# Two PSUM banks per head take turns under the attention scores of short query tiles

## The chip, the cores and the metric

The kernel runs on one core of one Trainium2 chip. The core has TensorE (PE; its weight loads are shown apart as PEld), VectorE (DVE), ScalarE (ACT), GpSimd (POOL), SyncE (SP) and DMA queues. Each engine has its own list of instructions, which it works through in the order written; semaphores are all that ties one engine to another. PSUM, into which TensorE writes, has eight banks of 512 float32 columns by 128 partitions. The metric is the device time of one execution in microseconds (us); smaller is better.

## The reference

One layer of a hybrid decoder trunk for two groups of requests: a prompt of 1024 tokens and eight sequences of four new tokens each. An input projection feeds an mLSTM group and a native-sparse-attention (NSA) group; their gated outputs are joined, projected and added back. The change is in the NSA part of the prompt. Cut to what matters:

```
scale = N_HEAD_DIM ** -0.5            # 64
s_c = einsum(q, k_compressed) * scale; p_c = masked_softmax(s_c)    # 64 compressed blocks
s_s = einsum(q_rot, k_selected) * scale; p_s = masked_softmax(s_s, pos_s <= t)
s_w = einsum(q_rot, k_window) * scale; p_w = masked_softmax(s_w, 0 <= t - s < 512)
out = g0 * (p_c @ v_c) + g1 * (p_s @ v_s) + g2 * (p_w @ v_w)
```

There are 8 query heads on 2 key/value heads of 64 dimensions. With 1024 prompt tokens there are 16 selection blocks of 64 and the top 16 are taken, so the selected branch is causal attention over everything up to the query. The window branch looks back 512 tokens.

## The kernel before

The whole kernel is one hand-ordered program per engine: projections of the prompt and the mLSTM recurrence (to about 560 us), compression of keys and values, the attention loop over the prompt (590 to 872 us), the part for the eight sampled sequences (to about 1070 us), and the output projection.

**Tiling of the attention loop.** The prompt is cut into 8 query tiles of 128 tokens. Each tile has 8 pairs; a pair p = 8i + 4br + g is tile i, branch br (0 selected, 1 window) and query head g of each of the two key/value heads h = 0, 1. Helper `pair(p)` gives nb, the number of 128-token key blocks: i + 1 for the selected branch, at most 5 for the window branch. So pairs 0 to 31 (tiles 0 to 3) have 1, 2, 3 and 4 blocks, and all from pair 32 on have five to eight.

**One pair, engine by engine.**
- TensorE, `scores(p)` (L2007 on): for each head one matmul of up to 512 key columns, from 64 of the 128 rows of the array (head 0 the lower, head 1 the upper), into the head's own PSUM banks, 2h and, above four blocks, 2h + 1 (L2019). A float32 matmul shows as two instructions, so a group for both heads is "x4". Then a small bf16 matmul adds the causal mask (L2025) and raises `s_done`.
- VectorE, `max_of` (L1515): the row maximum, negated, from PSUM.
- ScalarE, `exps` (L1134): exponentials from PSUM into SBUF `pp[p % 2][h]`, with the row sum, which is read out by a short instruction of its own (ACTIVATION_READ_ACCUMULATOR); this raises `s_exp`.
- VectorE, `scale` (L1524, L1526): reciprocal of the sum, then multiplication with it and the gate.
- TensorE, `turn_weights(p, h)` (L2038): one 128 x 128 transpose per block, into banks 4 and 5 in turn. ScalarE, `take_turned` (L1147), copies them to SBUF.
- TensorE, `values` (L2051): products with the values, accumulated in bank 6 over a tile. VectorE, `take_outputs` (L1533), multiplies the tile's result by its gate path.

**Order.** TensorE's list for step p is: scores(p + 1), turn_weights(p, 0), the start of a tile's accumulation with the compressed branch (L2070, at p % 8 = 2, after a wait for the last tile's take_outputs), half of the values of two pairs back, turn_weights(p, 1), and at steps 0, 1, 3 and 5 of a tile one of four parts of `aux`, which prepares the next tile's queries and compressed scores through bank 7. VectorE's list for step p: maxima of pair p + 1 for both heads, then scalings of pair p + 1 for both heads, plus the compressed branch's work at steps 1 and 2. ScalarE's: take_turned(p, 0), exponentials of pair p + 1 for both heads, take_turned(p, 1), plus a part of `aux` in four of the steps.

**The wait in question.** Before head h's first matmul of pair p TensorE waits for `s_exp` to reach 2p - 1 + h: the exponentials of the same head in the pair before must have read the bank.

Of the kernel before, what the change touches and what calls it, by code (L numbers as in the profile page):

```python
# [11 lines left out]
ALU = mybir.AluOpType  # L12
ACT = mybir.ActivationFunctionType
AX = mybir.AxisListType

P = 128
# [52 lines left out]
K_CAUSAL = K_ID + P  # L69
# [63 lines left out]
def first_tile(g):  # L133
    return MISC + sum(TILES[:g])


def tile_of(n):

    g = max(g for g in range(NG) if first_tile(g) <= n)
    return g, n - first_tile(g)  # L140
# [32 lines left out]
def build(nc, I, O):  # L173
    ctx = ExitStack()
    with ctx:
# [7 lines left out]
        masks = sb("masks", [P, K_MT], BF16)  # L183
# [20 lines left out]
        def bank(b, n=1):  # L204
            return PS[:, b * 512:(b + n) * 512]
# [64 lines left out]
        def from_xt(n):  # L270
            nonlocal o
            o += n
            assert o <= KC * TA
            return XT[:, o - n:o]
        pp_a = from_xt(3 * T).rearrange("p (s x) -> p s x", s=3)
        qz = from_xt(2 * GQ * P).rearrange("p (s g t) -> p s g t", s=2, g=GQ)
# [8 lines left out]
        nmax = from_xt(4)  # L285
# [5 lines left out]
        pp = [[pp_a[:, 0, :], pp_a[:, 1, :]], [pp_a[:, 2, :], MT[:, 4096:5120]]]  # L291
# [8 lines left out]
        ktr = KTR[:, :].rearrange("p (b t) -> p b t", b=2)  # L300
# [161 lines left out]
        s_exp = sem("s_exp")  # L462
# [79 lines left out]
        def pair(p):  # L542

            i, br, g = p // PAIRS, p // GQ % 2, p % GQ
            k0 = max(0, i - WB) if br else 0
            return i, br, g, k0, i + 1 - k0

        turn_count, turns = [], 0
        for p in range(NT * PAIRS):
            for h in range(KVH):  # L550
                turn_count.append(turns)
                turns += -(-pair(p)[4] // 4)
# [383 lines left out]
        def _(act):  # L936
# [69 lines left out]
            for u in range(8):  # L1006
                n = first_tile(u // 4) + 3 * (u % 4)
# [18 lines left out]
            for i in range(NT):  # L1026
                n = first_tile(3) + i
# [4 lines left out]
            for i in range(NT):  # L1032
                n = first_tile(4) + i
# [10 lines left out]
            for n in range(first_tile(5), first_tile(8)):  # L1044
                g, i = tile_of(n)
# [35 lines left out]
            for r in range(TILES[8]):  # L1081
                n = first_tile(8) + r
# [44 lines left out]
            def exps(p, h):  # L1127

                nb, u = pair(p)[4], 2 * p + h
                act.wait_ge(s_max, u + 1)  # L1130
                if p >= 2:

                    act.wait_ge(p_turned, turn_count[u - 3])
                nc.scalar.activation(pp[p % 2][h][:, 0:nb * P], bank(2 * h, 2)[:, 0:nb * P], ACT.Exp,  # L1134
                                     bias=nmax[:, u % 4:u % 4 + 1], accum_out=sums[:, u % 4:u % 4 + 1]).then_inc(s_exp, 1)

            def take_turned(p, h):

                i, br, g, k0, nb = pair(p)
                q = p // 2  # L1140
                if q >= 2:

                    act.wait_ge(pv_done, q - 1)
                for j in range(0, nb, 4):
                    n, y = min(4, nb - j), turn_count[2 * p + h] + j // 4
                    act.wait_ge(p_turned, y + 1)
                    nc.scalar.activation(pt[q % 2][:, h, j:j + n, g % 2 * P:(g % 2 + 1) * P],  # L1147
                                         bank(4 + y % 2)[:, 0:n * P].rearrange("p (k t) -> p k t", k=n), ACT.Copy)\
                        .then_inc(pt_ready, 1)
# [5 lines left out]
            for h in range(KVH):  # L1155
                exps(0, h)
            for p in range(NT * PAIRS):
                i = p // PAIRS
                take_turned(p, 0)
                if p + 1 < NT * PAIRS:  # L1160
                    for h in range(KVH):
                        exps(p + 1, h)
                take_turned(p, 1)
                if i + 1 < NT and p % PAIRS in ACT_AUX:
                    aux_act(i + 1, ACT_AUX.index(p % PAIRS))
# [60 lines left out]
            for i in range(NT + 1):  # L1226
                r = slice(0, P if i < NT else NS)
# [11 lines left out]
        def _(dve):  # L1239
# [102 lines left out]
            for i in range(NT):  # L1342
                n = first_tile(2) + i
# [3 lines left out]
            for i in range(NT):  # L1347
                n = first_tile(4) + i
# [4 lines left out]
                g = GM[:, i * DM:(i + 1) * DM]  # L1353
# [5 lines left out]
            for c in range(NT):  # L1359
# [12 lines left out]
                for h in range(MH):  # L1372
                    u = bank(h // 2)[:, h % 2 * 129:h % 2 * 129 + 129]
# [60 lines left out]
            for r in range(TILES[8]):  # L1434
                n = first_tile(8) + r
                b, t = bank(4 + n % 4), r % 3 * THIRD
                w = min(THIRD, T - t)
                g = gnt[:, r // 3, t:t + w]
                dve.wait_ge(ztanh, NT + r + 1)
                ins = nc.vector.scalar_tensor_tensor(g, g, 1.0, b[:, 0:w], op0=ALU.add, op1=ALU.mult)  # L1440
                if r % 3 == 2:
                    g = gnts[:, r // 3, :]
# [69 lines left out]
            def max_of(p, h):  # L1512
                nb, u = pair(p)[4], 2 * p + h
                dve.wait_ge(s_done, u + 1)
                nc.vector.tensor_reduce(nmax[:, u % 4:u % 4 + 1], bank(2 * h, 2)[:, 0:nb * P], AX.X, ALU.max,  # L1515
                                        negate=True).then_inc(s_max, 1)

            def scale(p, h):
# [19 lines left out]
            for h in range(KVH):  # L1538
                max_of(0, h)
            for h in range(KVH):  # L1540
                scale(0, h)
            for p in range(NT * PAIRS):
                i = p // PAIRS
                if p % PAIRS == 2 and i:
                    take_outputs(i - 1)
                if p + 1 < NT * PAIRS:
                    for h in range(KVH):
                        max_of(p + 1, h)
                    for h in range(KVH):
                        scale(p + 1, h)  # L1550
                if i + 1 < NT and p % PAIRS == SHIFT:
                    shift_compressed(i + 1)
                if i + 1 < NT and p % PAIRS == SUM:
                    sum_compressed(i + 1)
# [110 lines left out]
            for g in range(2):  # L1665
# [85 lines left out]
                for h in range(KVH):  # L1751
                    r = slice(h * ND, (h + 1) * ND)
                    src = bank(7)[0:ND, 0:P].rearrange("p (j h t g) -> p h g j t", j=4, h=KVH, t=ST)[:, h, :, :, :]
                    n = slice(g * 16, g * 16 + 16)
# [6 lines left out]
            for i in range(NT + 1):  # L1761
                p = slice(0, P if i < NT else NS)
                dve.wait_ge(y_sq, i + 1)
                r = yrs[p, i % 2:i % 2 + 1]
# [11 lines left out]
        def _(pe):  # L1776
            mm = nc.tensor.matmul
# [108 lines left out]
            for g, (name, c0, width) in enumerate(GROUPS):  # L1886
# [11 lines left out]
                for r in range(TILES[g]):  # L1898
                    n = first_tile(g) + r
# [75 lines left out]
            idb = masks[:, K_ID:K_ID + P]  # L1975
# [31 lines left out]
            def scores(p):  # L2007

                i, br, g, k0, nb = pair(p)
                if p % PAIRS == 0:  # L2010
                    pe.wait_ge(qz_ready, i + 1)
                old = br == 1 and i >= WB
                for j in range(0, nb, 4):
                    n = min(4, nb - j)
                    for h in range(KVH):
                        if p and j == 0:
                            pe.wait_ge(s_exp, 2 * p - 1 + h)
                        r = slice(h * ND, (h + 1) * ND)
                        mm(bank(2 * h + j // 4)[:, 0:n * P], qz[r, i % 2, g, :], ktr[r, br, (k0 + j) * P:(k0 + j + n) * P],  # L2019
                           start=True, stop=not (j + n == nb or (old and j == 0)))  # L2020
                for h in range(KVH):
                    if old:
                        mm(bank(2 * h)[:, 0:P], idb, masks[:, K_OLD:K_OLD + P], start=False, stop=nb > 4)
                    last = nb - 1
                    mm(bank(2 * h + last // 4)[:, last % 4 * P:(last % 4 + 1) * P], idb, masks[:, K_CAUSAL:K_CAUSAL + P],  # L2025
                       start=False, stop=True).then_inc(s_done, 1)

            def turn_weights(p, h):
# [28 lines left out]
            for part in range(4):  # L2057
                aux(0, part)
            scores(0)
            for p in range(NT * PAIRS):  # L2060
                i = p // PAIRS
                if p + 1 < NT * PAIRS:
                    scores(p + 1)
                turn_weights(p, 0)
                if p % PAIRS == 2:

                    pe.wait_ge(ptc_ready, i + 1)
                    if i:
                        pe.wait_ge(on_ready, i)
                    mm(bank(6), vc_bd, ptc, start=True, stop=False, skip_group_check=True).then_inc(oc_done, 1)  # L2070
                if p >= 2:
                    values(p // 2 - 1, p % 2)
                turn_weights(p, 1)
                if i + 1 < NT and p % PAIRS in AUX:
                    aux(i + 1, AUX.index(p % PAIRS))
# [212 lines left out]
```

## Time and profile before

| | |
|---|---|
| three runs, us | 1211.83, 1206.05, 1212.48 (median 1211.83) |
| the profiled execution | 1210.63 us, its span 1208.8 us |
| TensorE busy in the span | 1110.3 us (92%) |
| weight loads | 647.3 us (54%) |
| VectorE busy | 478.3 us (40%) |
| ScalarE busy | 325.1 us (27%) |
| attention loop over the prompt | 590 to 872 us |
| tiles 0 to 3 of it | 589.9 to 698.6 us |
| mean granted TensorE clock | 0.959 of 2.4 GHz |

The span is the time from the first to the last instruction in the profile. Busy time of TensorE counts from a matmul's start to its modelled end; neighbours overlap, and time in which one matmul of a group waits while the one before is still counted doesn't show as idle. The "idle before" of a group is the time in which the engine did nothing ahead of an instruction of it, and the name behind the arrow is what released it.

### The profile page before, as it was taken

The numbers are of one execution on the slowest core, as the hardware profiler recorded it, in microseconds if no ns is written. First come the engines' busy times: TensorE is split into PE (matmuls) and PEld (weight loads), VectorE is DVE, ScalarE is ACT, GpSimd is POOL, SyncE is SP. The second block draws the span as 40 slices with busy tenths as digits, with TensorE's granted clock in tenths as the row PEclk, the third lists the DMA queues.
The fourth block names the chain that finished last, engine by engine and source line by source line (L and its number), as shares of the span: only waits on it lengthen the run. The fifth ranks groups of instructions, "written<-read, shape, count | busy, mean of one in ns | idle before, by whom it ended". The sixth has DMA issues, their size and how long they took to land.

```text
span 1208.8 us, 14340 instructions
## 1 busy us (share of the span) xinstructions
PE 1110.3 (92%) x5319; PEld 647.3 (54%) x5319; DVE 478.3 (40%) x1025; ACT 325.1 (27%) x791; POOL 71.6 (6%) x180
## 2 busy tenths in 40 slices
PE   5999999999999999999789999999949868679997
PEld 3566644444455556866544566665636537244442
DVE  6443430001212222332467777777454443321121
ACT  4421100000011111101356666676531112001100
POOL 1000000000000011200100000010140011000000
PEclk9999999999999999999889999999977998779999
DMA  9202020303020514210310000000143533812221
GB/s 325 121 2 70 1 70 0 89 1 72 3 87 18 109 42 109 62 48 1 108 33 2 1 2 1 1 2 1 26 112 102 161 109 114 247 53 70 70 70 44
DMA packets 78685, 77.21 MB, mean 64 GB/s; under 512 B 28675, under 2 KB 63151, under 8 KB 78551
## 3 DMA queue, kind: packets, MB, share of 16 engines
q1 hardware_dynamic: 70150, 72.06, 19.6%
q10 hardware_dynamic: 8464, 4.23, 1.8%
q8 instruction: 42, 0.69, 0.2%
q14 instruction: 29, 0.23, 0.1%
HBM read 66.33 MB, written 14.10 MB: 67 GB/s over the span
## 4 chain that ended last, share of the span: by engine, by line
PE 78%; DVE 7%; SPq 7%; issue 4%; ACT 3%; DMA 2%; ACTq 0%; POOL 0%; DVEq 0%; POOLq 0%
PE PS L1911 25%; PE PS L1904 13%; PE PS L2253 10%; PE PS L2019 7%; PE PS L2038 5%; PE PS L2051 5%; SPq L678 3%; SPq L694 2%; SPq L687 1%; PE PS L2191 1%; PE PS L1955 1%; PE PS L2025 1%; ACT XT L1134 1%; PE PS L2144 1%; PE PS L2070 1%
## 5 line engine op out<-in xcount | busy, mean ns | idle before, releaser
L1911 PE MATMUL PS<-WR,XT 128*128 128x512 f32 (+1 forms) x768 | 306.9, 557 | 0.0
L1911 PEld LDWEIGHTS PS<-WR,XT 128*128 128x128 f32 x768 | 144.0, 190 | 147.7 <-issue 144.6
L1904 PE MATMUL PS<-XT,WR 128*128 128x352 f32 x576 | 172.2, 460 | 2.1 <-ACT QN L1015 2.1
L1904 PEld LDWEIGHTS PS<-XT,WR 128*128 128x128 f32 x576 | 108.8, 190 | 62.2 <-ACT QN L1015 2.7
L1515 DVE TENSOR_REDUCE XT<-PS 128x1 f32<-128x640 f32 (+7 forms) x128 | 84.5, 702 | 36.9 <-PE PS L2025 36.8
L2019 PE MATMUL PS<-KTR,XT 64*128 64x512 f32 (+3 forms) x384 | 92.5, 499 | 6.2 <-ACT XT L1134 5.6
L1134 ACT ACTIVATE XT<-PS,XT 128x640 f32<-128x640 f32 (+7 forms) x96 | 66.6, 701 | 10.7 <-DVE XT L1515 10.7
L2019 PEld LDWEIGHTS PS<-KTR,XT 64*128 64x128 f32 x384 | 45.5, 190 | 37.5 <-issue 17.0
L2038 PE MATMUL PS<-cst,XT 128*128 128x128 f32 x396 | 62.0, 281 | 0.8 <-ACT MT L1147 0.8
L2253 PE MATMUL PS<-WR,QT 128*128 128x512 f32 x128 | 57.6, 593 | 0.6 <-DVE XT L1755 0.6
L2253 PE MATMUL PS<-WR,KT 128*128 128x512 f32 x128 | 57.5, 592 | 0.0
L1526 DVE TENSOR_SCALAR XT<-XT,small 128x640 f32<-128x640 f32 (+7 forms) x96 | 53.5, 558 | 3.5
L1147 ACT ACTIVATE MT<-PS 128x512 f32<-128x512 f32 (+3 forms) x96 | 41.1, 465 | 47.7 <-PE PS L2038 47.6
L1147 ACT ACTIVATE VV<-PS 128x512 f32<-128x512 f32 (+3 forms) x96 | 41.3, 470 | 40.3 <-PE PS L2038 40.3
L2038 PEld LDWEIGHTS PS<-cst,XT 128*128 128x128 f32 x396 | 42.7, 142 | 13.7 <-issue 11.5
L1351 DVE SCALAR_TENSOR_TENSOR KTR<-KTR,PS 128x512 f32<-128x512 f32 x8 | 5.5, 687 | 104.1 <-ACT KTR L1038 104.1
L1765 DVE RECIPROCAL XT<-XT 128x1 f32<-128x1 f32 (+1 forms) x9 | 1.5, 163 | 103.1 <-ACT XT L1234 103.1
L1231 ACT ACTIVATE KTR<-PS 128x1024 f32<-128x1024 f32 (+1 forms) x9 | 9.2, 1022 | 120.6 <-PE PS L2253 120.6
L2253 PEld LDWEIGHTS PS<-WR,QT 128*128 128x128 f32 x128 | 24.2, 190 | 30.9 <-issue 30.9
L2253 PEld LDWEIGHTS PS<-WR,KT 128*128 128x128 f32 x128 | 24.3, 190 | 30.6 <-issue 30.6
L2191 PE MATMUL PS<-VV,XT 128*32 128x512 f32 x48 | 30.3, 750 | 9.7 <-DVE VV L1687 9.7
L2051 PE MATMUL PS<-MT,KVN 128*64 128x256 f32 x264 | 35.4, 394 | 0.8 <-ACT MT L1147 0.8
(440 smaller groups left out, 1291.1 us busy)
## 6 DMA issues: line engine op xcount, KB each, us to landing
WR<-in_w_in SPq DMA_DIRECT2D x24, 512.0 KB, 7.7
WR<-in_cache_kv_cmp SPq DMA_DIRECT2D x48, 128.0 KB, 2.5
MT<-row_factors ACTq DMA_DIRECT2D x16, 256.0 KB, 7.4
WR<-in_w_in SPq DMA_DIRECT2D x32, 128.0 KB, 3.4
KVN<-in_cache_kv_sel SPq DMA_DIRECT2D x32, 128.0 KB, 2.0
GM<-in_cache_kv_sel SPq DMA_DIRECT2D x32, 128.0 KB, 2.0
QN<-in_cache_kv_win SPq DMA_DIRECT2D x8, 512.0 KB, 5.5
XT<-in_x_prompt SPq DMA_DIRECT2D x8, 512.0 KB, 4.2
```

What stands on the lines that cost most here:

```text
L678: return sp.value_load(table[0:1, b * NPG + n:b * NPG + n + 1], min_val=0, max_val=I["cache_kv_cmp"].shape[1] - 1)
L1134: nc.scalar.activation(pp[p % 2][h][:, 0:nb * P], bank(2 * h, 2)[:, 0:nb * P], ACT.Exp, bias=nmax[:, u % 4:u % 4 + 1], accum_out=sums[:, u ...
L1147: nc.scalar.activation(pt[q % 2][:, h, j:j + n, g % 2 * P:(g % 2 + 1) * P], bank(4 + y % 2)[:, 0:n * P].rearrange("p (k t) -> p k t", k=n) ...
L1515: nc.vector.tensor_reduce(nmax[:, u % 4:u % 4 + 1], bank(2 * h, 2)[:, 0:nb * P], AX.X, ALU.max, negate=True).then_inc(s_max, 1)
L1526: nc.vector.tensor_scalar(pp[p % 2][h][:, 0:nb * P], pp[p % 2][h][:, 0:nb * P], s1, gates[:, i, gc:gc + 1], op0=ALU.mult, op1=ALU.mult).th ...
L1904: ins = mm(b[:, 0:THIRD], w[:, k, r // 3 * P:(r // 3 + 1) * P], xt[:, k, r % 3 * THIRD:(r % 3 + 1) * THIRD], **f)
L1911: ins = mm(b[:, 0:width], xt[:, k, r * P:(r + 1) * P], w[:, k, :], **f)
L2019: mm(bank(2 * h + j // 4)[:, 0:n * P], qz[r, i % 2, g, :], ktr[r, br, (k0 + j) * P:(k0 + j + n) * P], start=True, stop=not (j + n == nb or ...
L2038: ins = nc.tensor.transpose(bank(4 + y % 2)[:, k * P:(k + 1) * P], pp[p % 2][h][:, (j + k) * P:(j + k + 1) * P], ident)
L2051: ins = mm(bank(6)[h * ND:(h + 1) * ND, x], v, pt[q % 2][:, h, k, :], start=False, stop=br == 1 and k == nb - 1, skip_group_check=True)
L2191: ins = mm(bank(3 if br else q)[rows_j(j), :], qbd_rot[:, q_cols(j)], ktb[:, m % 2, q * 512:(q + 1) * 512], start=True, stop=True)
L2253: ins = mm(bank(i % 2 * 2 + half)[0:P if i < NT else NS, :], a, wo[:, c, half * 512:half * 512 + 512], start=c == 0, stop=c == KC - 1)
```

## The change

For pairs with up to four key blocks, a head's scores go to bank 2h in even pairs and bank 2h + 1 in odd ones. The wait before them is then for the exponentials of two pairs back (`2p - 3 + h`), which read the same bank. Maximum and exponentials read the bank that the new helper `score_bank` names. Pairs with five or more blocks use both banks as before and keep the old wait.

```diff
+        def score_bank(p, h):
+            return 2 * h + (p % 2 if pair(p)[4] <= 4 else 0)
...
-                nc.scalar.activation(pp[p % 2][h][:, 0:nb * P], bank(2 * h, 2)[:, 0:nb * P], ACT.Exp,
+                nc.scalar.activation(pp[p % 2][h][:, 0:nb * P], bank(score_bank(p, h), -(-nb // 4))[:, 0:nb * P], ACT.Exp,
...
-                nc.vector.tensor_reduce(nmax[:, u % 4:u % 4 + 1], bank(2 * h, 2)[:, 0:nb * P], AX.X, ALU.max,
+                nc.vector.tensor_reduce(nmax[:, u % 4:u % 4 + 1], bank(score_bank(p, h), -(-nb // 4))[:, 0:nb * P], AX.X, ALU.max,
...
-                        if p and j == 0:
+                        if j == 0 and nb > 4:
                             pe.wait_ge(s_exp, 2 * p - 1 + h)
+                        elif j == 0 and p >= 2:
+                            pe.wait_ge(s_exp, 2 * p - 3 + h)
                         r = slice(h * ND, (h + 1) * ND)
-                        mm(bank(2 * h + j // 4)[:, 0:n * P], qz[r, i % 2, g, :], ktr[r, br, (k0 + j) * P:(k0 + j + n) * P],
+                        mm(bank(score_bank(p, h) + j // 4)[:, 0:n * P], qz[r, i % 2, g, :], ktr[r, br, (k0 + j) * P:(k0 + j + n) * P],
...
-                    mm(bank(2 * h + last // 4)[:, last % 4 * P:(last % 4 + 1) * P], idb, masks[:, K_CAUSAL:K_CAUSAL + P],
+                    mm(bank(score_bank(p, h) + last // 4)[:, last % 4 * P:(last % 4 + 1) * P], idb, masks[:, K_CAUSAL:K_CAUSAL + P],
```

## Rows read from the trace of the kernel before

**Rows 1.** The page, sections 1 (busy, share, instructions) and 4 (chain by line).

```profile
PE 1110.3 (92%) x5319; PEld 647.3 (54%) x5319; DVE 478.3 (40%) x1025; ACT 325.1 (27%) x791; POOL 71.6 (6%) x180
...
PE PS L1911 25%; PE PS L1904 13%; PE PS L2253 10%; PE PS L2019 7%; PE PS L2038 5%; PE PS L2051 5%; SPq L678 3%; SPq L694 2%; SPq L687 1%; PE PS L2191 1%; PE PS L1955 1%; PE PS L2025 1%; ACT XT L1134 1%; PE PS L2144 1%; PE PS L2070 1%
```

**Rows 2.** Stretch, length, PE busy, PEld, DVE, ACT, POOL, clock, DMA share, GB/s.

```profile
589.90:610.60 20.70, 18.52 (x101) 12.30 (x100) 13.03 (x52) 11.28 (x49) 2.58 (x5) 0.73 0.35 108
610.60:636.10 25.50, 21.94 (x129) 11.73 (x128) 17.50 (x56) 14.44 (x53) 2.59 (x5) 0.93 0.04 12
636.10:665.40 29.30, 26.94 (x164) 14.76 (x164) 20.88 (x57) 18.00 (x53) 2.78 (x5) 1.00 0.01 1
665.40:698.60 33.20, 31.74 (x194) 17.03 (x192) 23.96 (x57) 21.15 (x53) 2.65 (x5) 1.00 0.00 1
698.60:866.00 167.40, 165.55 (x1169) 104.96 (x1167) 120.21 (x221) 113.52 (x269) 11.02 (x19) 1.00 0.00 1
```

**Rows 3.** PE lines, tiles 0-3: form, count, busy us, mean ns, idle.

```profile
L2019 PE MATMUL PS<-KTR,XT 64*128 64x128 f32 x32 | 6.6, 410 | 2.2 <-ACT XT L1134 2.1
...
L2019 PE MATMUL PS<-KTR,XT 64*128 64x256 f32 x32 | 7.5, 429 | 1.8 <-ACT XT L1134 1.7
...
L2070 PE MATMUL PS<-STG,cst 128*128 128x512 f32 x2 | 1.9, 1048 | 1.8 <-DVE KT L1533 1.8
...
L2019 PE MATMUL PS<-KTR,XT 64*128 64x384 f32 x32 | 9.8, 534 | 1.4 <-ACT XT L1134 1.1
...
L2019 PE MATMUL PS<-KTR,XT 64*128 64x512 f32 x32 | 11.5, 641 | 0.5 <-ACT XT L1134 0.5
```

**Rows 4.** Timeline, pair 21's scores: start, length, engine, line, form, count, idle before.

```profile
654.87 0.58 ACT L1134 ACTIVATE XT<-PS,XT 128x384 f32<-128x384 f32 x1 [1.27 <-DVE XT L1515]
...
655.59 1.47 PE L2019 MATMUL PS<-KTR,XT 64*128 64x384 f32 x4 [1.08 <-ACT XT L1134]
655.77 0.48 DVE L1526 TENSOR_SCALAR XT<-XT,small 128x384 f32<-128x384 f32 x1
655.90 0.20 ACT L1134 ACTIVATION_READ_ACCUMULATOR XT<-PS,XT 128x1 f32 x1
...
656.15 0.29 PEld L2019 LDWEIGHTS PS<-KTR,XT 64*128 64x128 f32 x2 [0.27 <-ACT XT L1134]
...
656.36 0.48 DVE L1526 TENSOR_SCALAR XT<-XT,small 128x384 f32<-128x384 f32 x1
...
657.12 0.50 PE L2038 MATMUL PS<-cst,XT 128*128 128x128 f32 x3
657.26 1.02 DVE L1515 TENSOR_REDUCE XT<-PS 128x1 f32<-128x384 f32 x2 [0.42 <-PE PS L2025]
```

**Rows 5.** Timeline around pair 5's scores, tile 0.

```profile
603.77 0.83 PE L2019 MATMUL PS<-KTR,XT 64*128 64x128 f32 x4 [1.30 <-ACT XT L1134]
...
603.95 0.35 DVE L1526 TENSOR_SCALAR XT<-XT,small 128x128 f32<-128x128 f32 x1
...
604.73 0.42 PE L2038 MATMUL PS<-cst,XT 128*128 128x128 f32 x1
```

**Rows 6.** Timeline: one short score group of each of tiles 0 to 3.

```profile
598.20 0.49 PE L2019 MATMUL PS<-KTR,XT 64*128 64x128 f32 x4
...
618.52 0.71 PE L2019 MATMUL PS<-KTR,XT 64*128 64x256 f32 x4
...
646.55 0.92 PE L2019 MATMUL PS<-KTR,XT 64*128 64x384 f32 x4
...
695.25 1.24 PE L2019 MATMUL PS<-KTR,XT 64*128 64x512 f32 x4
```

**Rows 7.** A stretch of tile 0, columns as in rows 2.

```profile
604.60:607.90 3.30, 3.30 (x18) 1.87 (x18) 1.87 (x9) 1.37 (x7) 0.00 (x0) 0.50 0.32 98
```

**Rows 8.** Timeline of SyncE's DMA issues, 600 to 872 us.

```profile
602.73 9.02 SPq L687 DMA_DIRECT2D XT<-in_cache_kv_cmp  x8
871.87 0.33 SPq L707 DMA_DIRECT2D MT<-sample_rows  x1
```

## The prediction

> **What bounds the kernel now.** I read the page first: PE is busy for 92% of the span and carries most of the chain, 7% of it on the score line L2019 [rows 1]. Then the span by stages: the attention loop runs from 590 to 872 us, and the change touches its first four query tiles alone, 589.9 to 698.6 us, 108.7 us in all; from tile 4 on every pair has five or more key blocks [rows 2]. In these four tiles PE shows 18.5, 21.9, 26.9 and 31.7 us busy of 20.7, 25.5, 29.3 and 33.2 us; VectorE and ScalarE are under 75% throughout [rows 2]. So PE's order of work bounds the stretch, with waits inside it.
>
> The groups of PE's lines in each tile say what stands before the scores: 2.2, 1.8, 1.4 and 0.5 us of idle time, 5.9 in all, nearly all released by the exponentials at L1134 [rows 3]. This is the visible part of the wait that the change removes. The other part is inside the score group. One pair shows it [rows 4]: head 0's matmuls start at 655.59, head 1's weight load only at 656.15, right after the accumulator read of head 1's exponentials ends at 656.10, and four matmuls take 1.47 us together. Where both heads' exponentials were long done, the same four take 0.92 us (tile 2), and 0.49, 0.71 and 1.24 us in tiles 0, 1 and 3 [rows 6]. The heads use different 64-row halves of the array; the traces show that they overlap once neither waits. PE counts as busy in both cases.
>
> **The change, part by part.**
> *The banks and the narrower reads.* Pairs 0 to 31 read and write the same number of columns from another bank. No instruction is added, removed or reordered, and no DMA. Cost nothing: the durations of reduce and exponential go by columns, which stay.
>
> *The wait.* Scores of pair p+1 waited for the exponentials of pair p; now for those of pair p-1. PE passed the transposes of pair p-1 just before, which waited for the scaled weights, hence for those exponentials: the new wait is always met already. Scores start as soon as PE is free. The first pair with five blocks still waits as before, and so does everything behind.
>
> First term, idle time before scores: 5.9 us [rows 3]. Second term, the group's own length: tiles 0 to 3 show 6.6, 7.5, 9.8 and 11.5 us for eight pairs each [rows 3]; eight overlapped ones would take 8 x 0.49 = 3.9, 8 x 0.71 = 5.7, 8 x 0.92 = 7.4 and 8 x 1.24 = 9.9 us [rows 6]. The differences are 2.7, 1.8, 2.4 and 1.6 us; in tile 0 about 0.3 of it is the half clock (1.2 GHz) of its first part rather than a wait, so 2.4. Sum of the second term 8.2 us, of both 14.1 us. This is the upper bound.
>
> *What is late next.* Behind the scores PE has the transposes of pair p, head 0 (L2038), which need the scaled weights (L1526). They can't move ahead of these. In [rows 4] the scaling ends at 655.77 + 0.48 = 656.25, a transpose could start 0.06 later, and starts at 657.12: 0.81 us to win, where idle time and length promised 1.08 + 0.55 = 1.63. In [rows 5] the scaling ends at 604.30 and the transpose starts at 604.73: 0.37 us to win where 1.30 + 0.35 were promised. The pattern returns before pairs 1, 9 and 13, each giving 0.55 to 0.7 us and losing 0.7. Taken off: 0.8 + 1.3 + 3 x 0.7 = 4.2 us. In the other pairs the transpose starts 0.3 us or more after the scaling, and their smaller excess fits. Left: 14.1 - 4.2 = 9.9 us; by tile about 2.3, 2.1, 3.0 and 2.5.
>
> *The second limit.* With scores out of the way a loop remains: both exponentials (654.87 to 656.10, 1.23 us), the second scaling (ends 656.84, 0.74 us), the maximum of the next pair (half of 1.02 us and about 0.1 to its reader), 2.6 us a pair in tile 2 [rows 4]. The tile takes 29.3 / 8 = 3.7 us a pair before, and 3.3 after: covered. In tiles 0 and 1 the instructions are shorter, but PE's work shrinks more; there the loop and PE are about equal, and I take off another 0.9 us for these two tiles, an estimate between 0 (the loop always hidden) and 3.5 (all that tiles 0 and 1 gain beyond 0.9). Forecast of the stretch: 9.9 - 0.9 = 9.0 us.
>
> *What passes through unchanged.* VectorE's take of the outputs (L1533) holds PE for 1.8 us in tile 1 [rows 3]; it hangs on the compressed scores, which PE issues earlier by as much as PE gains, so the hole moves along. Tiles 4 to 7 (698.6 to 866) start 9 us earlier and keep their length. SyncE issues nothing between 612 and 871.87, and its next one waits for the last output tile [rows 8], so what comes behind moves with it.
>
> The Trainium skill, "Perfetto Trace Analysis", section "Identifying the Most-Contended Engine", says that the busy share of matmuls doesn't tell how near TensorE is to its limit, and names the weight load's share instead. The busy matmuls leave only 1.5 us free in tile 3, the weight loads fill 17.0 of 33.2 us [rows 2]. Going by the matmuls' idle time alone, the gain would be the 5.9 us cut by the same transposes, 3.9 us; by the lengths in [rows 6] it is 9. I go by the lengths.
>
> **Against its own time.** The profiled execution took 1210.63 us with a span of 1208.8; 1.8 us lie around it. 1210.6 - 9.0 = 1201.6 us. The median of the three runs is 1211.83, 1.2 us above that execution, so 1202.8; I say 1202.5 us.
>
> **Rivals.**
> *A, the forecast:* 9 us gone, between 6 and 12.
>
> *B, only the idle time goes.* The overlap of the two heads doesn't come, since something other than the wait made the six short groups short. Against it: the head 1 weight load starts 0.05 us after the exponentials each time [rows 4]. Gain 3.9 us: 1208 us.
>
> *C, VectorE and ScalarE take over.* Each pair closes the loop through both, with copies of the transposes between the exponentials. For it: they are 0.71 and 0.61 busy in tile 2, 0.69 and 0.57 in tile 1 [rows 2], and all of it is one chain. Tiles 0 and 1 would give 0.9 instead of 3.5 and tile 2 half: 0.9 + 1.5 + 2.5 = about 5 us, 1207 us.
>
> *D, TensorE's clock falls, and the kernel is slower.* Tile 0 already ran at a mean clock of 0.73 and tile 1 at 0.93 [rows 2], with a stretch at 0.50 while PE's matmuls filled all of it [rows 7]. If run-ahead turns one long hole per pair into several small ones, and the clock stays at 1.2 GHz through tiles 0 and 1, 31 us more are at half rate (597.8 to 636.1 without the two slow stretches). Half of that, 15.5 us, is lost, less what hides in waits: 9 gained, 15 lost, 1218 us. It decides from 18 us more at half rate on, where the loss passes 9 us. Against it: holes shrink in sum, and in tiles 2 and 3 the mean clock was 1.00, the full 2.4 GHz, with holes of the same kind [rows 2, 3].
> The Trainium skill, "TensorE: Matmul & The Clock Gate", section "A second HAM failure mode: psum-queue depth-cycling", tells of kernels in which cycling through PSUM banks left TensorE with small pauses and an oscillating clock. By that rule this change would go D's way; the trace so far shows pauses without a fall in tiles 2 and 3 and doesn't bear it out.
>
> *E, more than forecast.* Fewer half-rate stretches in tiles 0 and 1, since PE has fewer holes there: 3.3 us at half rate return 1.65 us each; two of them, and all caps loose, give 13 us: 1199 us.
>
> *F, nothing.* Some part behind the loop has its own time and absorbs the gain, such as the state's loads and stores around 910 to 940 us: 1211 us. Against it: they too start after the last output tile.
>
> **How the numbers follow.** A 0.60, B 0.10, C 0.12, D 0.04, E 0.08, F 0.06. The likeliest gives 1202.5. A alone reaches from 1199 to 1206 and the three runs lie 6.4 us apart; with C, B and E at the ends the range is 1197 to 1209. About 0.5%, 6 us, is what a measurement of this kernel can tell from no change: faster means under 1205.8. A holds it to nine tenths (0.54), E whole (0.08), C and B to a third (0.07): 0.69 faster. Slower is D, 0.03 of its 0.04. The rest, 0.28, is within.
>
> **What would show it.** Score groups without idle time from L1134 in tiles 0 to 3, their lengths near 3.9, 5.7, 7.4 and 9.9 us by tile; the weight load of head 1 in one piece with head 0's. Pair 32's scores near 689.7 instead of 698.7. New idle time before L2038, released by L1526, about 4 us in sum: that is the cap. Tiles 4 to 7 at 167 us as before. It would be wrong if the score groups keep their 1.2 to 1.5 us (B), if idle time before L2038 reaches 8 us (C), if the clock rows show more of 0.50 before 640 us (D), or if the loop ends 9 us earlier and the kernel doesn't (F).

## The result: 1.1% faster, and the profile after

The changed kernel took 1198.73 us (median of 6 runs, 1192.72 to 1200.15) beside 1212.15 us for the kernel before (6 runs, 1206.05 to 1212.88): ratio 0.9893, 95% interval 0.9864 to 0.9922. That is 13.4 us less by the medians, where 9 were forecast. In a second comparison, on another chip, the ratio was 0.9913 (0.9886 to 0.9939), about 10.5 us. The two profiled executions differ by 11.2 us (spans 1208.8 and 1197.6). One execution of all those below, of the kernel with the heads one after the other (1249.68 us), ran in a slower state and is left out of its numbers.

The stretches of the changed kernel, tiles 0 to 3 and 4 to 7, then one of tile 1 (columns: stretch, its length, busy us of PE, PEld, DVE, ACT and POOL, clock, DMA share, GB/s):

```profile
589.90:609.50 19.60, 17.95 (x101) 11.40 (x100) 13.05 (x51) 11.26 (x49) 2.58 (x5) 0.71 0.36 106
609.50:631.30 21.80, 18.89 (x129) 10.27 (x128) 17.16 (x56) 14.42 (x53) 2.59 (x5) 1.00 0.07 21
631.30:657.70 26.40, 24.65 (x166) 13.09 (x164) 20.59 (x57) 18.18 (x55) 2.79 (x5) 1.00 0.01 2
657.70:687.80 30.10, 29.18 (x194) 15.65 (x192) 23.78 (x57) 21.11 (x53) 2.64 (x5) 1.00 0.00 1
687.80:855.20 167.40, 165.55 (x1169) 104.95 (x1167) 120.20 (x221) 113.54 (x269) 11.01 (x19) 1.00 0.01 1
621.70:625.00 3.30, 3.15 (x24) 1.59 (x22) 2.02 (x7) 1.95 (x6) 1.02 (x1) 1.00 0.00 0
```

Beside [rows 2]: the tiles went from 20.7, 25.5, 29.3 and 33.2 us to 19.6, 21.8, 26.4 and 30.1: 1.1, 3.7, 2.9 and 3.1 us, 10.8 in all. Tiles 4 to 7 take 167.4 us in both. All of the gain that the profiles show up to the loop's end lies in the stretch that the change touches.

TensorE's groups by line in the four tiles of the changed kernel (form, count, busy us, mean ns, idle before and its releaser; L2026 are the scores, L2045 the transposes of the weights, L2077 the start of a tile's accumulation):

```profile
L2026 PE MATMUL PS<-KTR,XT 64*128 64x128 f32 x32 | 5.2, 414 | 0.0
L2045 PE MATMUL PS<-cst,XT 128*128 128x128 f32 x11 | 4.1, 377 | 1.5 <-DVE XT L1530 1.5
...
L2026 PE MATMUL PS<-KTR,XT 64*128 64x256 f32 x32 | 5.6, 428 | 0.0
L2045 PE MATMUL PS<-cst,XT 128*128 128x128 f32 x24 | 5.2, 292 | 1.1 <-DVE XT L1530 1.1
L2077 PE MATMUL PS<-STG,cst 128*128 128x512 f32 x2 | 1.1, 630 | 1.8 <-DVE KT L1537 1.8
...
L2026 PE MATMUL PS<-KTR,XT 64*128 64x384 f32 x32 | 7.3, 535 | 0.0
L2045 PE MATMUL PS<-cst,XT 128*128 128x128 f32 x37 | 6.6, 283 | 0.7 <-DVE XT L1530 0.7
L2077 PE MATMUL PS<-STG,cst 128*128 128x512 f32 x2 | 1.1, 630 | 1.0 <-DVE KT L1537 1.0
...
L2026 PE MATMUL PS<-KTR,XT 64*128 64x512 f32 x32 | 9.0, 641 | 0.0
L2077 PE MATMUL PS<-STG,cst 128*128 128x512 f32 x2 | 1.1, 630 | 0.9 <-DVE KT L1537 0.9
```

Against [rows 3] the idle time before scores fell from 5.9 us to nothing, and the score groups from 6.6, 7.5, 9.8 and 11.5 us to 5.2, 5.6, 7.3 and 9.0, while the mean of one matmul (414, 428, 535, 641 ns) stayed where it was: the instructions are as long as ever, they lie on top of each other. In their place there is new idle time before the transposes, 3.3 us, released by the scaling (L1530).

The same spot as in [rows 4], pair 21, in the changed kernel's timeline (start, length, engine, line, form, count, idle before):

```profile
648.18 0.30 PEld L2026 LDWEIGHTS PS<-KTR,XT 64*128 64x128 f32 x4 [0.17 <-issue]
648.18 0.92 PE L2026 MATMUL PS<-KTR,XT 64*128 64x384 f32 x4
...
649.52 0.48 DVE L1530 TENSOR_SCALAR XT<-XT,small 128x384 f32<-128x384 f32 x1
649.65 0.20 ACT L1138 ACTIVATION_READ_ACCUMULATOR XT<-PS,XT 128x1 f32 x1
...
650.06 0.55 PE L2045 MATMUL PS<-cst,XT 128*128 128x128 f32 x3 [0.74 <-DVE XT L1530]
```

The scores start 1.7 us before head 1's exponentials of pair 20 are read out (648.18 against 649.65 + 0.20), with all four weight loads in one piece, and the group takes 0.92 us in place of 1.47. Then TensorE waits: the scaling ends at 650.00 and the transpose starts at 650.06, the 0.06 us that the cap was worked out with. And pair 5, as in [rows 5]:

```profile
602.18 0.49 PE L2026 MATMUL PS<-KTR,XT 64*128 64x128 f32 x4
...
603.72 0.35 DVE L1530 TENSOR_SCALAR XT<-XT,small 128x128 f32<-128x128 f32 x1
...
604.12 0.33 PE L2045 MATMUL PS<-cst,XT 128*128 128x128 f32 x1 [1.23 <-DVE XT L1530]
```

Most of the 1.30 us of idle time there has only moved behind the scores, where it is 1.23.

### The profile page after: what moved, and what is told of

It reads as the page before. It is cut to its first block, busy times and chain, and to the rows that moved or that the text cites. A ratio compares the mean times of both kernels' runs of the same rounds, so it can differ in the third digit from the quotient of the medians.

```text
span 1197.6 us, 14340 instructions
## 1 busy us (share of the span) xinstructions
PE 1104.4 (92%) x5319; PEld 642.6 (54%) x5319; DVE 477.7 (40%) x1025; ACT 325.1 (27%) x791; POOL 71.7 (6%) x180
## 4 chain that ended last, share of the span: by engine, by line
PE 84%; DVE 9%; ACT 3%; issue 2%; DMA 1%; SPq 0%; ACTq 0%; POOL 0%; DVEq 0%; POOLq 0%
PE PS L1915 25%; PE PS L1908 13%; PE PS L2260 10%; PE PS L2026 6%; PE PS L2045 5%; PE PS L2058 5%; PE PS L1959 3%; PE PS L2198 2%; PE PS L2194 1%; PE PS L1945 1%; DVE VV L1691 1%; PE PS L2032 1%; PE PS L2151 1%; PE PS L1913 1%; DVE XT L1530 1%
## 5 line engine op out<-in xcount | busy, mean ns | idle before, releaser
L2026 PE MATMUL PS<-KTR,XT 64*128 64x512 f32 (+3 forms) x384 | 84.3, 499 | 0.4 <-ACT XT L1138 0.2
L2045 PE MATMUL PS<-cst,XT 128*128 128x128 f32 x396 | 62.2, 281 | 4.2 <-DVE XT L1530 3.4
L2026 PEld LDWEIGHTS PS<-KTR,XT 64*128 64x128 f32 x384 | 39.8, 191 | 28.4 <-issue 17.9
L1530 DVE TENSOR_SCALAR XT<-XT,small 128x640 f32<-128x640 f32 (+7 forms) x96 | 53.5, 558 | 3.5
L2045 PEld LDWEIGHTS PS<-cst,XT 128*128 128x128 f32 x396 | 42.5, 142 | 17.8 <-issue 10.0
L2198 PE MATMUL PS<-VV,XT 128*32 128x512 f32 x48 | 32.8, 802 | 9.7 <-DVE VV L1691 9.7
```

The lines of the kernel that those rows point to most:

```text
L1530: nc.vector.tensor_scalar(pp[p % 2][h][:, 0:nb * P], pp[p % 2][h][:, 0:nb * P], s1, gates[:, i, gc:gc + 1], op0=ALU.mult, op1=ALU.mult).th ...
L2026: mm(bank(score_bank(p, h) + j // 4)[:, 0:n * P], qz[r, i % 2, g, :], ktr[r, br, (k0 + j) * P:(k0 + j + n) * P], start=True, stop=not (j + ...
L2045: ins = nc.tensor.transpose(bank(4 + y % 2)[:, k * P:(k + 1) * P], pp[p % 2][h][:, (j + k) * P:(j + k + 1) * P], ident)
L2198: ins = mm(bank(3 if br else q)[rows_j(j), :], qbd_rot[:, q_cols(j)], ktb[:, m % 2, q * 512:(q + 1) * 512], start=True, stop=True)
```

## Experiments

Each was timed over five rounds beside the kernel before. The first four shared a chip (kernel before: 1207.53 us median), the last four another (1207.85). The times expected for the first four were written around 1212 us, so the ratios tell more than the absolute times.

**Other banks, old wait.** The changed kernel with the first wait put back:

```diff
-                        if j == 0 and nb > 4:
+                        if p and j == 0:
                             pe.wait_ge(s_exp, 2 * p - 1 + h)
-                        elif j == 0 and p >= 2:
-                            pe.wait_ge(s_exp, 2 * p - 3 + h)
```

> Banks take turns as in the changed kernel, but head h's scores wait for the exponentials of the pair just before, as in the kernel before. Theory (the wait does all of it, the bank alone does nothing): as before, 1212 us within 3, tiles 0 to 3 at 108 to 109 us, 5 to 6 us of idle time before scores. Rival (reading the other bank or the narrower access is what helps): near 1199 us, tiles 0 to 3 at 98 us.

Measured: ratio 1.0009 (0.9981 to 1.0037), 1206.92 us. Its stretches, the same tiles, then the part from the loop's end to the output projection:

```profile
589.90:610.60 20.70, 18.55 (x101) 12.30 (x100) 13.09 (x52) 11.34 (x49) 2.58 (x5) 0.73 0.37 107
610.60:636.10 25.50, 21.89 (x129) 11.74 (x128) 17.49 (x57) 14.49 (x53) 2.59 (x5) 0.93 0.04 12
...
867.90:1073.90 206.00, 149.39 (x1007) 101.55 (x1007) 91.42 (x243) 36.71 (x85) 25.69 (x52) 0.86 0.45 128
```

The tiles repeat [rows 2] to 0.1 us. The banks by themselves do nothing; all of it is the wait.

**Heads one after the other.** The changed kernel, with head 0's mask between the two heads' scores:

```diff
                            start=True, stop=not (j + n == nb or (old and j == 0)))
+                        if nb <= 4:
+                            mm(bank(score_bank(p, h))[:, (nb - 1) * P:nb * P], idb, masks[:, K_CAUSAL:K_CAUSAL + P],
+                               start=False, stop=True).then_inc(s_done, 1)
-                for h in range(KVH):
+                for h in range(KVH if nb > 4 else 0):
```

> The changed kernel, but in pairs with up to four blocks each head's mask follows its own scores, so the two heads' score matmuls no longer stand next to each other and can't overlap; the early start stays. Theory (most of the gain is the overlap of the two heads): a group grows from 0.64, 0.85 and 1.06 us in tiles 1 to 3 to about twice that plus 0.1, the tiles lose 5 to 9 us each in tiles 2 and 3, and the kernel is at 1212 to 1222 us, no better than before. Rival (the gain is the idle time that went): 1199 to 1203 us.

Measured: ratio 1.0126 (1.0090 to 1.0162), slower than the kernel before; medians 1223.74 against 1207.53 us, above the 1212 to 1222 expected. The timeline of TensorE around one pair of tile 3, then stretches of this kernel, the last two being tiles 2 and 3:

```profile
703.41 1.12 PE L2026 MATMUL PS<-KTR,XT 64*128 64x512 f32 x2
704.47 0.23 PE L2029 MATMUL PS<-masks 128*128 128x128 bf16 x1
704.63 1.12 PE L2026 MATMUL PS<-KTR,XT 64*128 64x512 f32 x2
705.68 0.23 PE L2029 MATMUL PS<-masks 128*128 128x128 bf16 x1
```

```profile
584.60:635.80 51.20, 47.42 (x166) 28.74 (x165) 22.93 (x80) 18.37 (x72) 5.64 (x12) 0.50 0.22 63
635.90:722.00 86.10, 85.44 (x436) 41.40 (x435) 56.78 (x146) 47.67 (x135) 6.47 (x11) 1.00 0.00 1
...
652.00:684.00 32.00, 31.94 (x166) 15.65 (x164) 21.19 (x58) 18.06 (x55) 2.79 (x5) 1.00 0.00 1
684.00:722.10 38.10, 38.10 (x193) 18.25 (x192) 24.41 (x56) 20.88 (x53) 2.64 (x5) 1.00 0.00 1
```

For comparison one pair of tile 3 in the changed kernel:

```profile
684.57 1.13 PE L2026 MATMUL PS<-KTR,XT 64*128 64x512 f32 x4
685.64 0.29 PE L2032 MATMUL PS<-masks 128*128 128x128 bf16 x2
```

One head alone needs 1.06 us from its start to its mask (703.41 to 704.47); both together, overlapped, need 1.07 (684.57 to 685.64). Apart they cost 2.3 us a pair. That is also more than the 1.4 us (11.5 / 8) of the kernel before [rows 3], where the heads overlapped in part, so this experiment takes away more than the change had brought. What it shows is that the missing idle time before scores (0.4 us over the whole loop here) gives no gain without the overlap. A second thing shows: TensorE ran at 1.2 GHz from 584.6 to 635.8 us, 51 us on end, with matmuls covering 93% of it. This is what rival D described, brought about by other means, and it makes the 1.0126 partly a matter of the clock. But tiles 2 and 3, all at full clock, took 32.0 and 38.1 us, against 29.3 and 33.2 in [rows 2], and the fastest execution, 1215.83 us at a mean clock of 0.968, is still slower than the kernel before at 0.968 (1202.49 to 1206.77 us).

**Overlap without an early start.** The kernel before, head 0 waiting for both heads' exponentials:

```diff
-                            pe.wait_ge(s_exp, 2 * p - 1 + h)
+                            pe.wait_ge(s_exp, 2 * p if p < 32 else 2 * p - 1 + h)
```

> The kernel before, but head 0's scores of pairs 1 to 31 wait for the exponentials of both heads of the pair before, so that the heads' matmuls overlap but start later. Theory (the end of a score group is set by head 1's start, so a late head 0 costs nothing): groups of 0.64, 0.85, 1.06 us, more idle time before them (about 14 us in place of 5.9), same time as before, 1212 us within 3. Rival (overlap by itself, without an early start, frees TensorE): 3 to 8 us faster than before.

Measured: ratio 1.0020 (1.0000 to 1.0041), 1209.88 us. Its score line over the loop (as in rows 3), and pair 21 in its timeline:

```profile
L2019 PE MATMUL PS<-KTR,XT 64*128 64x512 f32 (+3 forms) x376 | 83.4, 502 | 13.3 <-ACT XT L1134 10.1 <-ACT MT L1134 2.8
```

```profile
656.69 0.20 ACT L1134 ACTIVATION_READ_ACCUMULATOR XT<-PS,XT 128x1 f32 x1
656.94 0.30 PEld L2019 LDWEIGHTS PS<-KTR,XT 64*128 64x128 f32 x4 [1.88 <-ACT XT L1134]
656.94 0.92 PE L2019 MATMUL PS<-KTR,XT 64*128 64x384 f32 x4 [1.65 <-ACT XT L1134]
```

The groups are as short as in the changed kernel (0.92 us) and the busy time with them, and nothing is won: what shrank as busy time came back as idle time, 13.3 us of it. Short groups were worth something in this kernel only because they start early.

**Head 0 alone early.** The changed kernel, head 1 with the old wait:

```diff
-                            pe.wait_ge(s_exp, 2 * p - 3 + h)
+                            pe.wait_ge(s_exp, 2 * p - 3 + h if h == 0 else 2 * p)
```

> The changed kernel, but head 1 of pairs 2 to 31 keeps the old wait; head 0 alone starts early. Theory (both masks and both maxima come behind head 1, so its wait sets the pace): 1210 to 1212 us, 0 to 2 us below the kernel before. Rival (each head's wait is worth half): about 1205 us.

Measured: ratio 1.0009 (0.9986 to 1.0032), 1208.20 us. From its timeline, tile 2:

```profile
657.97 0.64 PEld L2025 LDWEIGHTS PS<-KTR,XT 64*128 64x128 f32 x4 [0.17 <-issue]
657.97 1.25 PE L2025 MATMUL PS<-KTR,XT 64*128 64x384 f32 x4
658.05 0.21 ACT L1138 ACTIVATION_READ_ACCUMULATOR MT<-PS,XT 128x1 f32 x1
```

The group ends 0.96 us after the read-out of head 1's exponentials (658.26 to 659.22), as in the kernel before. Head 1's wait sets the pace; taking away head 0's alone gave nothing.

**Tiles 2 and 3 alone.** `score_bank` alternates for three and four blocks only, and pairs up to 16 keep the old wait.

```diff
-            return 2 * h + (p % 2 if pair(p)[4] <= 4 else 0)
+            return 2 * h + (p % 2 if 3 <= pair(p)[4] <= 4 else 0)
...
-                        if j == 0 and nb > 4:
+                        if j == 0 and p and (nb > 4 or p <= 16):
```

> The changed kernel, but banks take turns and scores start early in tiles 2 and 3 alone; tiles 0 and 1 keep the old wait. Theory (the gain is local to each tile): tiles 0 and 1 as before, 20.7 and 24 to 25.5 us, tiles 2 and 3 as changed, 26.4 and 30.1 us; about 6 us below the kernel before. Rival (the gain of tile 1 was the clock that tiles 2 and 3 don't touch, and the whole is mostly that): under 4 us.

Measured: ratio 0.9942 (0.9918 to 0.9965), 1200.24 us, 7.6 us below the kernel before by the medians. Its stretches:

```profile
589.90:611.30 21.40, 19.34 (x101) 12.70 (x100) 13.34 (x53) 11.56 (x50) 2.58 (x5) 0.67 0.39 104
611.30:635.10 23.80, 20.17 (x129) 11.20 (x128) 17.23 (x56) 14.34 (x51) 2.60 (x5) 1.00 0.04 12
635.10:661.80 26.70, 24.91 (x164) 13.39 (x164) 20.64 (x57) 17.93 (x53) 2.79 (x5) 1.00 0.01 2
661.80:691.90 30.10, 29.18 (x194) 15.66 (x192) 23.79 (x57) 21.12 (x53) 2.64 (x5) 1.00 0.00 1
```

Tiles 2 and 3 have the changed kernel's lengths to 0.3 us, and 2.6 and 3.1 us, 5.7 in all, are gained there: the gain is local. Tile 1, with the old wait, takes 23.8 us here and not 25.5, since the clock is at 1.00 throughout; tile 0, with the old wait too, takes 21.4 us at a clock of 0.67 in place of 20.7 at 0.73. The time at half rate (1.2 GHz) in the two tiles, worked out from these means, is about 14 us in both kernels (14.1 and 14.7); it only lies elsewhere.

**The changed kernel again.**

> The changed kernel once more, for a second trace and a ratio beside the versions of this call. Theory (10.8 us come from the loop, the 2 us beyond it in the first comparison are the spread of executions): tiles 0 to 3 again 98 us or a little more if a half-rate stretch falls into tile 1, ratio to the kernel before 0.989 to 0.992. Rival (something behind the loop gains too): the part from the loop's end to the output projection is again shorter than in the kernel before by 2 us or more.

Measured: 1197.57 us, ratio 0.9913 (0.9886 to 0.9939). Tiles 0 to 3 take 97.8 us. The part behind the loop took 206.4 us in this execution, 209.9 in the first profile of the changed kernel, 210.3 in the one of the kernel before and 206.0 with the old wait put back (above). The rival's sign came, since 206.4 us is 3.9 less than in the kernel before. But the old wait shows 206.0 and the changed kernel's first profile 209.9: the part varies by 4 us whichever kernel ran, at a mean clock of 0.80 to 0.86, and that something there gains isn't borne out.

**VectorE takes the outputs first.** The changed kernel with one call moved, out of step 2:

```diff
-                if p % PAIRS == 2 and i:
-                    take_outputs(i - 1)
...
+                if p % PAIRS == 1 and i:
+                    take_outputs(i - 1)
                 if i + 1 < NT and p % PAIRS == SHIFT:
                     shift_compressed(i + 1)
```

> The changed kernel, and VectorE takes the last tile's outputs (L1537) at the end of step 1, ahead of the compressed scores' shift, in place of step 2, behind it. Theory (the idle time before L2077, 4.4 us in sum, is VectorE's order): that idle time falls under 1 us, 3 us less than the changed kernel. Rival (the shift comes later and holds the aux transposes or the next maxima): no change within 1 us, with idle time moved to L2045.

Measured: 1190.55 us, ratio to the kernel before 0.9878 (0.9843 to 0.9913). Its groups over the loop:

```profile
L2045 PE MATMUL PS<-cst,XT 128*128 128x128 f32 x396 | 62.3, 281 | 4.4 <-DVE XT L1530 3.5 <-ACT MT L1151 0.8
...
L2077 PE MATMUL PS<-STG,cst 128*128 128x512 f32 x16 | 8.3, 598 | 0.3 <-DVE KT L1537 0.3
```

Idle time before L2077 fell from 4.4 to 0.3 us and that before L2045 stayed (4.2 us in the changed kernel). So the hole that the prediction let pass through unchanged came from VectorE's list, in which taking the outputs stood behind the compressed scores' work. The loop took 262.6 us against 267.1 and 267.2 in the two profiles of the changed kernel.

**And the sum of the compressed branch a step later.** As above, with

```diff
-        AUX, ACT_AUX, SHIFT, SUM = [0, 1, 3, 5], [0, 2, 3, 5], 1, 2
+        AUX, ACT_AUX, SHIFT, SUM = [0, 1, 3, 5], [0, 2, 3, 5], 1, 3
```

> As v2_take_first, and VectorE sums the compressed exponentials at step 3 in place of step 2, so that the maxima of pair 4 of a tile don't wait for it. Theory: idle time before L2045 of 3.5 us in tiles 0 to 3 falls to about 2, 1 us less than v2_take_first, 4 us less than the changed kernel. Rival (the sum delays the pair behind just as much): as v2_take_first.

Measured: 1193.46 us, ratio to the kernel before 0.9878 (0.9850 to 0.9906), so not to be told from the version before it by time. Its groups over the loop:

```profile
L2045 PE MATMUL PS<-cst,XT 128*128 128x128 f32 x396 | 62.0, 281 | 3.7 <-DVE XT L1530 2.8 <-ACT MT L1151 0.8
...
L2077 PE MATMUL PS<-STG,cst 128*128 128x512 f32 x16 | 8.3, 598 | 0.3 <-DVE KT L1537 0.3
```

The loop took 259.7 us. Of the 2.9 us below the version before it, tile 0 gives 1.1 (no second half-rate stretch came in this execution), and tiles 1 to 5 give 1.8 with the clock at full. Idle time before L2045 fell by 0.7 us, not the 1.5 expected. Both versions beat the changed kernel in the profile (by 4.5 and 7.4 us in the loop); by the ratios, whose intervals overlap its own, that isn't settled.

## Why the prediction was right, and where it was short

**The bound and the wait.** TensorE's order bounded the stretch and the new wait is always met: no score in tiles 0 to 3 waits for ScalarE any more, and with the old wait put back all of the gain is gone. Right.

**First and second term.** 5.9 us of idle time went; the groups shrank by 1.4, 1.9, 2.5 and 2.5 us, 8.3 in all, where 8.2 were worked out. By tile it was off. Tile 0 gave 1.4 and not 2.4: its clock was still at a mean of 0.71, and part of its groups ran at 1.2 GHz, with or without a wait. Tile 3 gave 2.5 and not 1.6: the overlapped group of four blocks takes 1.13 us (9.0 / 8), and the example of 1.24 us in [rows 6] perhaps still held a rest of the wait, which isn't shown. The two errors cancelled. The prediction's gains by tile don't follow from its own terms either: tile 0 comes to 2.6 us after the cap, not 2.3, and tile 3 to 0.5 + 1.6 = 2.1, not 2.5; the sum of 9.9 is right.

**The cap.** 4.2 us were taken off for scores that can't push the transposes ahead of the scaling. The profile after has that as idle time before L2045: 1.5, 1.1 and 0.7 us, 3.3 in all. Right in place and mechanism, 0.9 us too large.

**The second limit.** Taken off: 0.9 us, an estimate. The parts measured add up to 5.9 + 8.3 - 3.3 = 10.9 us, and 10.8 went, but the match is partly luck. By tile the parts give 2.1, 2.6, 3.2 and 3.0 us, and the tiles shrank by 1.1, 3.7, 2.9 and 3.1. In tile 0 other lines grew, L1994 and L2008 from 3.3 us (L1990 and L2004 before) to 4.0, at a mean clock of 0.71; in tile 1 others shrank by more than that, for the reason below. C is out: tile 2 gave 2.9 us and not 1.5, and the idle time before the transposes is 3.3 us where 8 would have been its sign. A limit of the size of the 0.9 us isn't shown, nor ruled out.

**What was missing: a half-rate stretch.** The kernel before ran tile 1 at a mean clock of 0.93; a stretch of it in full:

```profile
621.70:625.00 3.30, 3.30 (x10) 0.71 (x9) 1.35 (x5) 1.01 (x4) 0.00 (x0) 0.50 0.00 0
```

It fell on the long matmuls of L2070 (1.9 us for two, [rows 3], and 1.1 in the changed kernel). The changed kernel's row for the same time has 1.00. With the old wait in tile 1 and the clock at full the tile takes 23.8 us (tiles 2 and 3 alone), with the stretch in place 25.5 (twice: kernel before and old wait put back). So of tile 1's 3.7 us, 2.0 are the wait and 1.7 the clock. The wait's own gain is then 10.8 - 1.7 = 9.1 us, beside 9.0 forecast. By tile it is 1.1 + 2.0 = 3.1 us in tiles 0 and 1, where 3.5 were forecast, and 6.0 in tiles 2 and 3, where 5.5 were: the closeness of the sum is better than that of its parts. The clock's part was rival E's mechanism, priced there at 1.65 us for each such stretch, and I had given it 0.08.

Is the clock's part luck or the change? In five profiles the scores of tiles 0 and 1 still wait for the pair before, at least for head 1: the kernel before, the old wait, both heads waiting, head 0 alone early, and tiles 2 and 3 alone. Their mean clocks from 580 to 650 us are 0.88, 0.88, 0.88, 0.85 and 0.88. The two profiles of the changed kernel and those of its two versions with another order on VectorE have 0.90, 0.90, 0.90 and 0.93. Over 70 us, 0.02 of the clock is about 3 us less at half rate (0.02 x 70 x 2), one stretch like the one above. So the gain of the clock came with the early scores in these nine profiles, and only where the stretch lies differs. The tenth, with the heads one after the other, starts early too and has 0.63, so the early start isn't enough by itself. Why the stretch goes is open. Neither the hole of 1.8 us at L2070 [rows 3] nor the one of 0.83 before pair 9, which the change takes away, decides it: with tiles 2 and 3 alone both are there (1.79 and 0.83 us), and tile 1 ran at full clock.

**The rest of the 13.4 us.** The profiled executions differ by 11.2, of which 10.8 lie in the four tiles and 0.4 behind the loop. The medians differ by 13.4 in one comparison and the ratio says 10.5 in the other, and each interval holds 11. The last 2 us of the first comparison lie within the spread of executions, in which the part behind the loop alone moves by 4 us; they aren't traced further.

**The other rivals.** B fell with the lengths of the score groups in the changed kernel itself; its 3.9 us had no working. D did not happen in the changed kernel (clock 0.71 in tile 0 against 0.73, 1.00 in tile 1 against 0.93). F fell: tiles 4 to 7 kept their length and what follows moved along. The chances given to the rivals add up to 0.90, those of faster, slower and within to 1.00, so a tenth belongs to no rival.

The Trainium skill, "TensorE: Matmul & The Clock Gate", section "A second HAM failure mode: psum-queue depth-cycling", tells of a kernel whose clock oscillates with short pauses as it cycles through PSUM banks. Here the banks taking turns with the old wait left the clock at 0.73 and 0.93, as before, and with the new wait the idle time was less and the clock higher.

The Trainium skill, "Perfetto Trace Analysis", section "Identifying the Most-Contended Engine", says that the busy share of matmuls is no good measure of how near TensorE is to its limit. The trace agrees: in four tiles about 8 us of it were waits inside groups. The experiment with both heads waiting shows the other side, that less busy time isn't less time either.

## What to carry to other kernels

A group of matmuls that waits in its middle counts as busy: compare the same group's length where its inputs were early, and take the difference as idle time. What a removed wait gives is the smaller of that and the slack of the next instruction's own input, worked out pair by pair against the instruction behind. Here the sum came within 0.1 us, with errors of 0.4 to 1 us in its parts that cancelled. Double-buffering helped here only when every part of the group was freed: freeing one head of two, or aligning both without starting them earlier, gave nothing.

## What the runs showed of the hardware

- Two float32 matmuls from different 64-row halves of the array, into different banks, take no longer together than one alone: 1.07 us to the next instruction for both with four blocks, 1.06 us for one.
- A half-rate stretch can last through work without a gap: with the heads one after the other the clock stayed at 1.2 GHz for 51 us, from 592.3 us on matmuls covered all of the 43.5 us that were left of it, and it rose at 635.8 us in the middle of such work.
- The same program runs a tile at different mean clocks from one execution to another: tile 0 with the old wait took 20.7 us at 0.73 and 21.4 at 0.67.
- The part behind the loop took between 206.0 and 210.3 us in four executions of three kernels that are the same there.
